# Hybrid decoder layer: dense units in another order, the convolution read from PSUM, and 21 slots for the expert stream instead of 19

## The chip, the cores and the metric

The kernel runs on one core of one Trainium2 chip. The metric is device time in microseconds (us) of one execution. TensorE (PE), VectorE (DVE), ScalarE (ACT) and GpSimd (POOL) compute; SyncE (SP) issues nearly all transfers from device memory. Each engine works through its own instructions in order and waits on semaphores.

## The reference, cut to what matters

One layer on 256 tokens of 1024 channels, float32 in and out:

```python
mod = silu(c) @ w_ada + b_ada                    # sh1, sc1, gt1, sh2, sc2, gt2
h = rmsnorm(x, norm1) * (1 + sc1) + sh1
q, k, v, ml_qk, ml_v, ml_o, ml_if, g_a, g_m = split(h @ w_in)
y_a = diff_attention(q, k, v)                    # 4 heads, softmax 0 minus lam * softmax 1, causal, ALiBi
qk = silu(sum(xp[:, j:j + S] * conv_w[j] for j in range(4)) + conv_b)   # causal, over time
h_t = mlstm(*split(qk), ml_v, gates)             # 4 heads
y_m = rmsnorm(sigmoid(ml_o) * h_t, mlstm_norm)
merged = sigmoid(g_a) * (y_a @ w_br_a) + sigmoid(g_m) * (y_m @ w_br_m)
x = x + gt1 * (merged @ w_out)
h2 = rmsnorm(x, norm2) * (1 + sc2) + sh2
# router: best of 4 groups, in it the best 2 of 8 experts; expert: w_e2 @ (silu(w_e1 h2) * (w_e3 h2))
x = x + gt2 * hier_moe(h2)
return rmsnorm(x, norm_f)
```

All weights are read once: the layer moves 164 MB, 100 MB of it for the 32 experts.

## The kernel before, in words

**Units.** All weights travel as units of 1 MB (128 partitions x 2048 float32), listed by `unit_list` (lines 55 to 69): 16 for the first phase (`mod` and `block`, 768 KB, in turn), then 40: `ada(i)` is a sixth of `w_ada` in four units, the rest are dense matrices. Each goes to a fixed slot of a ring of ten (`place`), and SP issues it once the last user of that slot is done (line 428). 96 expert units follow, eight quads of four experts, 12 units a quad: w1, w3, w2 of each. The first 19 go to slots freed by named jobs (`RELEASES`, lines 127 to 130), which include homes other than the ring (`late`, `qkT`, `gm`, `mqk`, `hT`, three spare tiles of `his`). Each later one waits until `used` counts one more consumed unit (line 440) and goes to the slot that comes next in the same cycle.

**Dense products** run in two rounded halves. For a dense unit d, ScalarE writes the high part (`split(d)`, line 502: 128 x 2048, one instruction), GpSimd subtracts it from the weight in four parts of 512 columns (line 478), and TensorE multiplies three times: high by high, low by high, high by low (`product`, line 1306: 48 products for a unit). `proj_T` and `proj` are its two layouts; `ml` is the mLSTM's q/k input (four units), `mv` its values, `mo` its output gate, `ga` and `gm` the branch gates. Three tiles hold high parts, so split(d) waits for unit d-3 to be consumed. `ada` (line 1259) is a float32 product of the conditioning vector in four column groups.

**Order by hand.** There is no planner: each engine's block lists its work. TensorE, from the end of the first phase: `if`, scores(0), ada(3), ifT, scores(1), ml0, scores(2), ml1, scores(3), ada(4), ml2, ml3, `cols` and `Mb` (the mLSTM's decay terms, which wait for `grows`), mv0, transposes of attention heads 0 and 1, mv1, `rb`, ada(2), times_v, mo0, mo1, ga0, ga1, gt1 spread, the mLSTM with ga2 and ga3, gm, branches, ada(5), `wo`, router. ScalarE's block has the splits between its own work: split(8), split(9) and split(10) around the copy of the four q/k banks (line 535); then for each head the exps, the copy of `ml` from its bank into `raw` and split(11 + h). VectorE's block: lam, scores and combine by head (lines 884 to 899), with conv(0) before combine(2) and conv(1) before combine(3), `cols`, conv(2), conv(3). A job in PSUM takes the next of eight banks in the order of `JOBS`, and its first product waits until the bank's last job is released.

**Convolution.** conv(i), lines 907 to 910: for each of two channels groups one TENSOR_SCALAR (last tap and bias), then three multiply-adds of `raw` shifted by one to three columns into `mqk`, each waiting for the one before.

**Experts.** quad(): up w1 (line 1644), gather half 0 of the next quad's tokens (line 1612), scatter the last quad's outputs into four accumulator banks (line 1601), gather half 1, up w3, transposes of the gate matrix and hidden values (lines 1619, 1622), down w2 (line 1656) into two banks. up runs four experts in turn on four column groups of the array; down runs two pairs of experts one after the other:

```python
for pair in ((0, 1), (2, 3)):
    wt = {e: arrived("w2", e, r, j) for e in pair}
    for c in range(2):
        for f in range(2):
            for e in pair:
```

The accumulators start as x (four products with the identity, line 1690), issued between the two gathers of the first quad.

## Time and profile before

| | us |
|---|---|
| median of 3 runs | 498.64 (496.84 to 499.54) |
| profiled execution | 499.77 |
| its span, first to last instruction | 497.9 |
| busy PE / DVE / ACT / POOL | 424.3 / 180.8 / 181.1 / 159.0 |
| mean granted clock of TensorE | 0.926 |
| DMA | 164.32 MB, mean 330 GB/s |

Busy times are unions of an engine's instructions, so a busy TensorE may still run at its lower clock: the granted clock is 1.00 at 2.4 GHz and 0.50 at 1.2 GHz. In rows of a timeline the columns are start, duration, engine, line, operation, output and inputs, count; brackets hold the idle time just before and what ended it.

### The profile page before, as it was taken

How to read it: one execution, taken by the hardware profiler on the slowest of the kernel's cores; microseconds unless marked ns; L12 is line 12 of the kernel's file. 1: busy time of each engine (PE TensorE's matmuls, PEld its weight loads, DVE VectorE, ACT ScalarE, POOL GpSimd, SP SyncE). 2: the span in 40 equal slices, each digit the busy share in tenths (PEclk: the TensorE clock that was granted, in tenths of full speed). 3: DMA queues.
4: the chain of work that ended last, by engine and by line, in shares of the span. 5: the costliest groups of instructions: out<-in, count | busy, mean ns of one | idle time of the engine just before them, and what ended most of it. 6: DMA issues, size and time to landing. Idle time of an engine off the chain costs nothing.

```text
span 497.9 us, 8612 instructions
## 1 busy us (share of the span) xinstructions
PE 424.3 (85%) x3612; PEld 317.9 (64%) x3612; DVE 180.8 (36%) x365; ACT 181.1 (36%) x332; POOL 159.0 (32%) x126
## 2 busy tenths in 40 slices
PE   6599459998599999999997989898989788584983
PEld 5599328898399999997996645363626254251531
DVE  0987027999661422357236011111111111102014
ACT  4676145654258357543343321212122112030122
POOL 0799074877335775997600000000000000000000
PEclk9799859999599999999996999898989889799799
DMA  8999988794096427477998299999999999999932
GB/s 296 424 419 421 422 352 355 280 378 168 9 406 223 151 105 254 170 274 318 424 420 339 74 387 423 421 421 420 421 420 421 421 423 420 421 423 419 419 157 86
DMA packets 23657, 164.32 MB, mean 330 GB/s; under 512 B 2624, under 2 KB 2752, under 8 KB 4928
## 3 DMA queue, kind: packets, MB, share of 16 engines
q1 hardware_dynamic: 23184, 162.15, 80.3%
q10 hardware_dynamic: 432, 1.57, 0.9%
q8 instruction: 31, 0.51, 0.4%
q14 instruction: 10, 0.08, 0.0%
HBM read 162.67 MB, written 1.05 MB: 329 GB/s over the span
## 4 chain that ended last, share of the span: by engine, by line
PE 59%; DMA 20%; DVE 14%; ACT 3%; issue 2%; SPq 1%; DVEq 0%; ACTq 0%
PE bank L1306 13%; PE cs_b L1644 10%; PE bank L1656 7%; PE cs_b L1306 7%; DMA ring<-in_rest 7%; PE bank L1612 6%; DMA hT<-in_e 6%; DMA his<-in_e 6%; PE bank L1601 4%; DVE mqk L910 3%; PE bank L1259 2%; PE bank L1349 2%; DMA ring<-in_mod 2%; DVE xn L897 1%; PE cs_b L1601 1%
## 5 line engine op out<-in xcount | busy, mean ns | idle before, releaser
L478 POOL TENSOR_TENSOR ring_r<-ring,his_r 128x512 fp32r<-128x512 f32 x120 | 158.6, 1357 | 74.7 <-ACT his_r L502 74.7
L715 ACT ACTIVATE raw<-bank,sm 128x128 f32<-128x128 f32 x72 | 27.1, 457 | 160.1 <-PE bank L1612 160.1
L502 ACT ACTIVATE his_r<-ring 128x2048 fp32r<-128x2048 f32 (+1 forms) x32 | 57.6, 1798 | 42.7 <-DMA ring<-in_rest 23.9
L1644 PE MATMUL cs_b<-ring,raw 128*32 128x256 f32 x544 | 58.5, 405 | 2.5 <-DMA ring<-in_e 2.5
L1185 DVE TENSOR_TENSOR tmp<-cs_b,tmp 128x256 f32<-128x256 f32 x8 | 3.4, 425 | 122.6 <-ACT tmp L723 122.6
L1612 PEld LDWEIGHTS bank<-const,xn 128*128 128x128 f32 x288 | 35.9, 199 | 9.0 <-issue 7.8
L1644 PE MATMUL cs_b<-his,raw 128*32 128x256 f32 x208 | 36.1, 420 | 5.5 <-DMA hT<-in_e 5.5
L1656 PE MATMUL bank<-ring,WT 128*32 128x512 f32 x128 | 39.2, 657 | 1.5 <-DVE WT L1190 1.5
L1644 PEld LDWEIGHTS cs_b<-ring,raw 128*32 128x32 f32 x544 | 29.4, 116 | 16.9 <-issue 6.3
L1612 PE MATMUL bank<-const,xn 128*128 128x128 f32 x288 | 37.7, 286 | 1.1 <-DVE const L1136 1.1
L1196 DVE TENSOR_TENSOR v<-bank,att 128x512 f32<-128x512 f32 x16 | 10.3, 687 | 48.1 <-PE bank L1656 48.1
L1306 PE MATMUL bank<-his_r 128*128 128x256 f32 x192 | 27.4, 286 | 0.0
L1601 PE MATMUL bank<-v,const 128*128 128x512 f32 x54 | 24.7, 594 | 1.7 <-DVE sm L1216 1.7
L1306 PEld LDWEIGHTS bank<-his_r 128*128 128x128 f32 x192 | 24.5, 190 | 1.1 <-issue 1.1
L1259 PE MATMUL bank<-ring,sm 128*32 128x256 f32 x256 | 18.7, 456 | 7.5 <-DVE sm L941 7.5
L1644 PEld LDWEIGHTS cs_b<-his,raw 128*32 128x32 f32 x208 | 16.8, 120 | 10.2 <-issue 8.6
L910 DVE SCALAR_TENSOR_TENSOR mqk<-raw,const,mqk 128x256 f32<-128x256 f32 x24 | 21.9, 913 | 0.9
L1656 PE MATMUL bank<-his,WT 128*32 128x512 f32 x56 | 19.7, 633 | 1.6 <-DVE WT L1190 1.6
L1259 PEld LDWEIGHTS bank<-ring,sm 128*32 128x32 f32 x256 | 9.1, 130 | 16.3 <-DVE sm L941 7.6
L1306 PE MATMUL cs_b<-his_r 128*128 128x256 f32 x128 | 18.4, 287 | 1.0 <-ACT his_r L662 1.0
L1656 PEld LDWEIGHTS bank<-ring,WT 128*32 128x32 f32 x128 | 9.4, 119 | 15.3 <-issue 13.0
L1644 PE MATMUL cs_b<-mqk,raw 128*32 128x256 f32 x48 | 13.0, 432 | 6.3 <-DMA his<-in_e 6.3
(385 smaller groups left out, 861.2 us busy)
## 6 DMA issues: line engine op xcount, KB each, us to landing
ring<-in_e SPq DMA_DIRECT2D x50, 1024.0 KB, 22.3
ring<-in_rest SPq DMA_DIRECT2D x40, 1024.0 KB, 7.0
his<-in_e SPq DMA_DIRECT2D x20, 1024.0 KB, 25.1
ring<-in_block SPq DMA_DIRECT2D x8, 768.0 KB, 21.3
late<-in_e SPq DMA_DIRECT2D x6, 1024.0 KB, 23.7
qkT<-in_e SPq DMA_DIRECT2D x5, 1024.0 KB, 18.7
mqk<-in_e SPq DMA_DIRECT2D x5, 1024.0 KB, 26.3
gm<-in_e SPq DMA_DIRECT2D x5, 1024.0 KB, 26.1
```

The lines of the kernel that those rows point to most:

```text
L478: pool.tensor_tensor(ring_r[:, slot_of(n), sl], ring[:, slot_of(n), sl], hi(d)[:, sl].bitcast(F32), ALU.subtract).then_inc(s["w_lo"], 1)
L502: act.activation(hi(d)[:, 0:WIDTH[d]], ring[:, slot_of(n), 0:WIDTH[d]], ACT.Copy).then_inc(s["w_hi"], 1)
L715: ins = act.activation(xg[:, b, k, :], token_bank[:, j * P:(j + 1) * P], ACT.Identity, bias=S("B2", KD)[:, k:k + 1], scale=S("A2", KD)[:, ...
L910: ins = dve.scalar_tensor_tensor(out=mqk[:, k, :], in0=raw[:, k, j:j + T], scalar=col("conv_w", 8 * j + k), in1=mqk[:, k, :], op0=ALU.mult ...
L1196: ins = dve.tensor_tensor(outs2[:, sl], out_banks[c][:], gt2b[:, sl], ALU.mult)
L1259: ins = pe.matmul(ps[32 * u:32 * u + 32, 0:256], S("cs", 8)[:, k:k + 1].to_broadcast([P, 32]), w[:, k - k0, 256 * u:256 * u + 256], start= ...
L1306: ins = pe.matmul(out, left(k), right(k), start=(i == 0 and k == 0), stop=(i == 2 and k == nk - 1))
L1349: ins = pe.matmul(pb(f"qk{i // 2}")[:, (i % 2) * T:(i % 2 + 1) * T], w[:, i * P:(i + 1) * P], h, start=start and i % 2 == 0, stop=stop, sk ...
L1601: ins = pe.matmul(y_banks[2 * tt + c][:], ptg[:, b, tt, :], outs2[:, 512 * c:512 * c + 512], start=False, stop=stop, skip_group_check=True)
L1612: ins = pe.matmul(token_bank[:, j * P:(j + 1) * P], xn[:, tt, k * P:(k + 1) * P], pone[:, tt].rearrange("p a n -> p (a n)"), start=(tt == ...
L1644: ins = pe.matmul(up_bank[e * CAP:(e + 1) * CAP, half], xg[:, b, k, e * CAP:(e + 1) * CAP], wt[e][:, k, :], start=(k == 0), stop=(k == KD ...
L1656: ins = pe.matmul(out_banks[c][e * CAP:(e + 1) * CAP, :], hidT[:, f, e * CAP:(e + 1) * CAP], wt[e][:, f, 512 * c:512 * c + 512], start=(f ...
```

## The change

- Units and TensorE's order: ml0 with scores(0) to ml3 with scores(3), ifT, mv0, mv1, ada(3), mo0, turn of ada(3), transposes of heads 0 and 1, `cols`, `Mb`, ada(4), mo1, times_v(0), (1), transposes of heads 2 and 3, ga0, times_v(2), (3), turn of ada(4), ada(2), ga1, `rb`; from the gt1 spread on as before. `JOBS` follows it.
- ScalarE and VectorE follow the new order (below). `scores` now has a buffer for each head (`sc` fills all of `att`), the mixes' factor on the second softmax goes to ScalarE (`scale`), and `wts` and `aT` move to `raw`, which is free.
- The convolution's last tap and bias are ScalarE's (`tap`, from the bank); its other three taps are VectorE's, with the bank as the first input. `raw` and its zero pad are no longer used for it.
- At the start normalize(0) goes ahead of modulation(0), and VectorE squares the last quarter of x.
- Two more slots for the expert stream: `OG` (the buffer of `o` with the gt1 spread next to it), freed when the squares of the new x are taken (`sq2`), and the home of x, freed when the normalized copy is made (`x2n`) and the accumulators hold x (`y_set`). The accumulators' four products go ahead of the gt2 spread.
- down() waits for all four w2 units and takes four experts in turn.

```diff
-    units = [u for k in range(KD) for u in (("mod", k), ("block", k))] + ada(3)
-    units += w_in(C_MQK, 2) + ada(4) + w_in(C_MQK + 512, 2)
-    units += w_in(C_MV, 2) + ada(2) + w_in(C_MO, 2) + w_in(C_GA, 4)
-    units += w_in(C_GM, 4)
+    units = [u for k in range(KD) for u in (("mod", k), ("block", k))]
+    units += w_in(C_MQK, 4) + w_in(C_MV, 2) + ada(3) + w_in(C_MO, 1) + ada(4) + w_in(C_MO + 256, 1)
...
+XSLOTS = SLOTS + 7
 YSLOTS = 16
...
-             (HT, "lg")]
+             (HT, "lg"), (OG, "sq2"), (X_HOME, "x2n")]
...
+        o_att = sb("o_att", [4096])
+        o, att = o_att[:, 0:1024].rearrange("p (t n) -> p t n", t=TT), o_att[:, 1024:4096]
         WT = sb("WT", [2, 384])
...
-        sc = att[:, 0:1536].rearrange("p (b c n) -> p b c n", b=2, c=2)
+        sc = att[:].rearrange("p (h c n) -> p h c n", h=HEADS, c=2)
...
                 return late[:, 0:UNIT]
+            if i == OG:
+                return o_att[:, 0:UNIT]
...
-                if n == NFIRST:
+                if n == NFIRST + 1:
...
-                elif job:
+                elif job == "sq2":
+                    sp.wait_ge(s["sq2"], 1)
+                elif job == "x2n":
+                    sp.wait_ge(s["x2n"], TT)
+                    sp.wait_ge(s["y_set"], 1)
+                else:
                     sp.wait_ge(*full(job))
                 load(slot_of(NPRE + m), m // QU, m % QU)
...
-                    act.wait_ge((xT0_in, xT1_in)[i // 2], 16)
+            for i in range(3):
+                act.wait_ge((xT0_in, xT1_in)[i // 2], 16)
...
-            split(9)
             for i in range(4):
                 act.wait_ge(*full(f"qk{i}"))
                 release(act.activation(qkT[:, 2 * i:2 * i + 2, :], pb(f"qk{i}")[:].rearrange("p (a n) -> p a n", a=2),
...
+            split(9)
+            act.wait_ge(s["lam_e"], 1)
+            act.activation(S("lexp", 2), S("ldot", 2), ACT.Exp).then_inc(s["lexp"], 1)
...
+                    act.activation(mqk[:, k, :], pb(f"ml{i}")[:, a * T:(a + 1) * T], ACT.Identity, bias=col("conv_b", k),
+                                   scale=col("conv_w", 24 + k)).then_inc(s["tap"], 1)
...
+                    act.activation(sc[:, h, 1, a:b], sc[:, h, 1, a:b], ACT.Identity, bias=0.0,
+                                   scale=S(f"rZl{h}", 2)[:, i:i + 1]).then_inc(s["sc1"], 1)
...
+            for h in range(HEADS):
+                tap(h)
+                split(10 + h)
+                exps(h)
+            split(14)
+            act.wait_ge(s["gates"], 2)
+            act.activation(grow[0:4, 2, :], grow[0:4, 2, :], ACT.Exp).then_inc(s["gexp"], 1)
+            act.wait_ge(s["gexp"], 1)
+            act.activation(grow[0:4, 2, :], grow[0:4, 2, :], ACT.Ln, bias=1.0).then_inc(s["gln"], 1)
+            scale(0)
+            scale(1)
+            values(0)
+            split(15)
+            scale(2)
+            values(1)
+            split(16)
+            scale(3)
+            output_gate(0)
+            split(17)
...
+            output_gate(1)
+            split(18)
             copy_a(2)
-            split(17)
             copy_a(3)
...
+            dve.wait_ge(xT1_in, 16)
+            dve.tensor_tensor(squares[:, 6:8, :], hT[:, 6:8, :], hT[:, 6:8, :], ALU.mult).then_inc(s["sq_d"], 1)
+            dve.wait_ge(*full("ss"))
+            release(dve.tensor_scalar(r1b, pb("ss")[:, 0:T], 1.0 / D, EPS, ALU.mult, ALU.add), "ss")
+            dve.wait_ge(s["std"], 1)
+            link(dve.reciprocal(r1b, r1b))
+            normalize(0)
...
             modulation(0, 0)
...
             modulation(0, 1)
...
+                    dve.wait_ge(s["sc1"], 2 * h + i + 1)
+                    dve.scalar_tensor_tensor(out=a_sb[:, h, a:b], in0=sc[:, h, 0, a:b], scalar=S(f"rZ{h}", 4)[:, i:i + 1],
+                                             in1=sc[:, h, 1, a:b], op0=ALU.mult, op1=ALU.add).then_inc(s["a_r"], 1)
...
+                dve.wait_ge(s["tap"], 2 * i + 2)
+                for a in range(2):
+                    k, seq = 2 * i + a, pb(job)[:, a * T:(a + 1) * T]
                     for j in range(3):
-                        ins = dve.scalar_tensor_tensor(out=mqk[:, k, :], in0=raw[:, k, j:j + T],
-                                                       scalar=col("conv_w", 8 * j + k), in1=mqk[:, k, :],
+                        back = 3 - j
+                        ins = dve.scalar_tensor_tensor(out=mqk[:, k, back:T], in0=seq[:, 0:T - back],
+                                                       scalar=col("conv_w", 8 * j + k), in1=mqk[:, k, back:T],
                                                        op0=ALU.mult, op1=ALU.add)
...
+                release(ins, job)
+
+            for h in range(HEADS):
+                conv(h)
+                scores(h)
+            gate_inputs()
+            dve.wait_ge(s["lexp"], 1)
+            link(dve.tensor_tensor(S("nlam", 1), S("lexp", 2)[:, 1:2], S("lexp", 2)[:, 0:1], ALU.subtract))
+            link(dve.tensor_scalar(S("nlam2", 1), S("nlam", 1), -LAMBDA_INIT, None, ALU.add))
+            sums(0)
+            sums(1)
+            mix(0)
+            sums(2)
+            mix(1)
             rows(3)
-            scores(0)
-            gate_inputs()
+            gate_sums()
+            sums(3)
+            mix(2)
+            mix(3)
...
-            scores(1)
-            combine(0)
-            scores(2)
-            gate_sums()
-            combine(1)
-            rows(4)
-            scores(3)
-            conv(0)
-            combine(2)
-
...
+            rows(4)
+            columns(A2, 4)
...
-            conv(2)
-            conv(3)
...
-            scores(0)
-            ada(3)
+            for h in range(HEADS):
+                proj_T(f"ml{h}", hsrc, next_dense(8))
+                if h == 0:
+                    for i in range(4):
+                        pe.wait_ge(*free(f"qk{i}"))
+                scores(h)
             ps = take("ifT")
             pe.wait_ge(*free("if"))
...
-            scores(1)
+            proj("mv0", hsrc, next_dense(8))
+            proj("mv1", hsrc, next_dense(8))
+            ada(3)
+            proj("mo0", hsrc, next_dense(8))
             ada_turn(3)
-            proj_T("ml0", hsrc, next_dense(8))
-            scores(2)
-            proj_T("ml1", hsrc, next_dense(8))
-            scores(3)
-            ada(4)
-            proj_T("ml2", hsrc, next_dense(8))
-            proj_T("ml3", hsrc, next_dense(8))
-            ada_turn(4)
...
+            transpose_a(0)
+            transpose_a(1)
...
-            proj("mv0", hsrc, next_dense(8))
-
+            ada(4)
+            proj("mo1", hsrc, next_dense(8))
...
-            transpose_a(0)
-            transpose_a(1)
-            proj("mv1", hsrc, next_dense(8))
...
+            po = [take("o0"), take("o1")]
+            times_v(0)
+            times_v(1)
+            transpose_a(2)
+            transpose_a(3)
+            gate_a(0)
+            times_v(2)
+            times_v(3)
+            ada_turn(4)
+            ada(2)
+            gate_a(1)
...
-            ada(2)
-            po = [take("o0"), take("o1")]
-            times_v(0)
-            times_v(1)
-            transpose_a(2)
-            proj("mo0", hsrc, next_dense(8))
-            transpose_a(3)
-            times_v(2)
-            proj("mo1", hsrc, next_dense(8))
-            times_v(3)
...
+            for job in ("x2T1", "wo3", "x2T2", "x2T3"):
+                pe.wait_ge(*free(job))
+            for tt in range(TT):
+                for c in range(2):
+                    ins = pe.matmul(y_banks[2 * tt + c][:], ident, x[:, tt, 512 * c:512 * c + 512], start=True, stop=False,
+                                    skip_group_check=True)
+            ins.then_inc(s["y_set"], 1)
             ada_spread(5, 2, 0)
             ada_spread(5, 2, 1)
...
-                for pair in ((0, 1), (2, 3)):
-                    wt = {e: arrived("w2", e, r, j) for e in pair}
-                    for c in range(2):
-                        for f in range(2):
-                            for e in pair:
-                                ins = pe.matmul(out_banks[c][e * CAP:(e + 1) * CAP, :], hidT[:, f, e * CAP:(e + 1) * CAP],
-                                                wt[e][:, f, 512 * c:512 * c + 512], start=(f == 0), stop=(f == 1),
-                                                tile_position=(0, e * CAP))
-                                if c == 1 and f == 1:
-                                    ins.then_inc(used, 1)
+                wt = [arrived("w2", e, r, j) for e in range(QUAD)]
+                for c in range(2):
+                    for f in range(2):
+                        for e in range(QUAD):
+                            ins = pe.matmul(out_banks[c][e * CAP:(e + 1) * CAP, :], hidT[:, f, e * CAP:(e + 1) * CAP],
+                                            wt[e][:, f, 512 * c:512 * c + 512], start=(f == 0), stop=(f == 1),
+                                            tile_position=(0, e * CAP))
+                            if c == 1 and f == 1:
+                                ins.then_inc(used, 1)
...
-            start_y(0)
             pe.wait_ge(s["g_evac"], 1)
             gather(1)
-            start_y(1)
```

## Rows read from the trace of the kernel before

**Rows 1.** The page, part 2: busy share of DMA in 40 slices of the span

```profile
DMA  8999988794096427477998299999999999999932
```

**Rows 2.** Windows: us, busy PE, PEld, DVE, ACT, POOL (count), clock, DMA share, GB/s

```profile
54.00:162.00 108.00, 88.16 (x792) 76.50 (x791) 67.15 (x123) 55.13 (x101) 59.01 (x46) 0.89 0.71 283
162.00:262.00 100.00, 98.34 (x850) 95.87 (x849) 37.79 (x67) 48.28 (x75) 67.14 (x51) 0.99 0.69 266
262.00:279.00 17.00, 14.41 (x64) 10.32 (x66) 8.21 (x45) 6.36 (x16) 0.00 (x0) 0.73 0.56 233
272.00:283.00 11.00, 11.00 (x96) 6.69 (x96) 1.61 (x6) 4.29 (x9) 0.00 (x0) 0.89 0.02 6
283.00:478.00 195.00, 165.71 (x1531) 88.82 (x1529) 25.58 (x56) 35.74 (x79) 0.00 (x0) 0.92 1.00 414
```

**Rows 3.** Timeline of TensorE

```profile
68.09 0.55 PE L1392 MATMUL cs_b<-qkT 64*128 64x128 f32 x1 [12.36 <-ACT qkT L535]
...
90.45 3.66 PE L1259 MATMUL bank<-ring,sm 128*32 128x256 f32 x64
...
129.60 5.62 PE L1259 MATMUL bank<-ring,sm 128*32 128x256 f32 x56 [7.48 <-DVE sm L941]
```

**Rows 4.** Chain of waits: start, duration, what

```profile
69.75 5.29 PE bank L1259 x64
75.05 4.92 DMA ring<-in_rest
...
129.60 6.05 PE bank L1259 x64
...
156.31 5.72 PE bank L1306 x48
...
278.97 3.65 PE cs_b L1644 x64
...
433.60 27.58 DMA his<-in_e
...
480.59 5.43 PE bank L1656 x32
```

**Rows 5.** Timeline of ScalarE

```profile
60.67 1.91 ACT L502 ACTIVATE his_r<-ring 128x2048 fp32r<-128x2048 f32 x1 [11.69 <-DMA ring<-in_rest]
```

**Rows 6.** Timeline of all engines at the start

```profile
14.54 1.75 DVE L827 RECIPROCAL tmp<-tmp 128x256 f32<-128x256 f32 x1
...
16.33 2.55 DVE L811 TENSOR_TENSOR hT<-hT,tmp 128x512 f32<-128x512 f32 x2
...
18.04 1.19 PE L1349 MATMUL bank<-his_r 128*128 128x256 f32 x4 [6.26 <-ACT his_r L520]
```

**Rows 7.** Windows, columns as in rows 2

```profile
79.70:82.10 2.40, 2.40 (x22) 2.40 (x21) 2.29 (x7) 2.10 (x2) 0.11 (x1) 1.00 1.02 430
...
129.50:133.10 3.60, 3.50 (x36) 1.66 (x40) 2.16 (x9) 3.09 (x9) 0.00 (x0) 0.50 0.00 0
```

**Rows 8.** Timeline of GpSimd

```profile
81.99 10.30 POOL L478 TENSOR_TENSOR ring_r<-ring,his_r 128x512 fp32r<-128x512 f32 x8 [9.50 <-ACT his_r L502]
...
102.60 5.43 POOL L478 TENSOR_TENSOR ring_r<-ring,his_r 128x512 fp32r<-128x512 f32 x4 [3.37 <-ACT his_r L502]
```

**Rows 9.** Timeline of VectorE

```profile
89.95 0.56 DVE L884 SCALAR_TENSOR_TENSOR att<-cs_b,const 128x384 f32<-128x384 f32 x1
...
104.08 4.23 DVE L910 SCALAR_TENSOR_TENSOR mqk<-raw,const,mqk 128x256 f32<-128x256 f32 x3
...
136.51 1.53 DVE L910 SCALAR_TENSOR_TENSOR mqk<-raw,const,mqk 128x256 f32<-128x256 f32 x3
```

**Rows 10.** Timeline of all engines before the first quad

```profile
268.52 3.78 PE L1612 MATMUL bank<-const,xn 128*128 128x128 f32 x16 [1.08 <-DVE const L1136]
...
272.09 3.06 PE L1690 MATMUL bank<-x,const 128*128 128x512 f32 x4
...
274.98 1.95 PE L1612 MATMUL bank<-const,xn 128*128 128x128 f32 x16
```

175 lines of the change are left out of this document (63 added, 112 removed).

## The prediction, made before the changed kernel ran

> **What bounds the kernel now.** I read the page first, then windows by stage, then the chain of waits, then the timelines of the places that the chain names. The DMA line of the page [rows 1] is to be read as three parts: full at the left, half empty in the middle, full from about 283 us on. The windows [rows 2] say what fills each part. From 54 to 162 us TensorE works 88.16 of 108 us at a granted clock of 0.89: time is lost here. From 162 to 262 us it works 98.34 of 100 us: nothing but less work would shorten this, and whatever is saved ahead of it is carried through. From 262 to 279 us the router leaves it gaps and a clock of 0.73. From 272 to 283 us DMA moves nothing (share 0.02), and from 283 to 478 us it is full (share 1.00, 414 GB/s) while TensorE is busy 165.71 of 195 us: the expert stream is bound by DMA. The chain agrees: its last DMA piece ends at 461.2 us, and behind it lie one quad's TensorE work and the final norm [rows 4]. So the end is: when the stream restarts, plus the units still to be moved, plus this tail.
>
> In the lossy stretch the timeline of TensorE shows two holes [rows 3]: 12.36 us before scores(0), released by ScalarE's copy of the q/k banks, and 7.48 us before ada(2), put down to the copy of `cols` on VectorE. ScalarE came late because its in-order queue stood 11.69 us at split(8) for the landing of ml0's weights [rows 5], which were fetched behind the four ada(3) units. VectorE came late because convolution and attention mixes lie ahead of `cols` in its order. After both holes the clock is at its lower level: ada(3) took 5.29 us and ada(2) 6.05 [rows 4], where ada(4), with no hole before it, took 3.66 [rows 3].
>
> **The change, part by part.**
>
> *Start.* normalize(0) goes ahead of modulation(0), which now waits behind sum, root and reciprocal. On VectorE: reciprocal from 12.7 instead of 14.54 us (1.75), one normalize (half of 2.55), then both modulations (2 x 1.2, by their spacing in time), and ScalarE's 1.1 us to the first hi tile: first product at 18.9 to 19.5 us, now 18.04 [rows 6]. The first six-bank pass is bound by TensorE from there on, so this is +1.0 us. Bounds: -0.5 (if the earlier square on VectorE and the shorter hole help) and +1.5.
>
> *Order of the dense units.* ml0 to ml3, mv0, mv1 come first, ada(3), ada(4), ada(2) later. ml0 now lands four units (10 us) earlier, before ScalarE asks for it at 50 us (it landed at 60.7 [rows 5]); the q/k copies stand ahead of split(9); TensorE goes from the `if` product straight to ml0, whose low part GpSimd has ready at 57 us. The hole of 12.4 goes and with it the cold clock behind it (1.7 on ada(3), 0.7 on scores(0)). In the ml part a head costs TensorE 5.72 [rows 4] + 0.9 = 6.6 us; VectorE six conv steps of 0.5 plus the scores' 2.3 [rows 7] = 5.3; ScalarE two taps, a split of 1.91 [rows 5] and four exps = 4.6; GpSimd 5.2 to 5.4 for a low part [rows 8]. All fit, GpSimd by half a microsecond. Attention then runs well ahead: I get `grows` on VectorE at about 104.4 us and `cols` on TensorE at 105.5, so the hole of 7.5 and its cold clock (2.4 on ada(2)) go too. Together -24.7 us.
>
> What is late next: split(17) (ga1) stands ahead of copy_a(0) on ScalarE. ga1's slot is freed by the end of ada(4), a landing in an idle queue takes 4.92 [rows 4], the split 1.91, the copy 0.5: 7.4 us, in which TensorE does mo1 (5.72). A hole of 1.7 us before times_v(0). Then copy_a(2) stands behind eight exps (ScalarE works 3.09 in the window 129.5 to 133.1 [rows 7]), two table loads and split(18): 9.0 us, against 7.8 of TensorE's work: a hole of 1.2. +2.9 us together (0 to 8: a wait behind the queue of each split). Behind these, o, rb and gt1 are ready about 1.4 us before TensorE wants them. VectorE now waits in columns(A2) for the turn of ada(4), 15 us earlier in its queue than the turn comes; behind it stand rows(2), o's scaling and rbias, none needed before ada(2) ends.
>
> *Convolution from PSUM.* ScalarE writes the last tap and bias, VectorE adds three taps read from the bank; the pad, the copy into `raw` and eight TENSOR_SCALARs go. Trace: three conv steps on `raw` in SBUF took 4.23 us (1.40 each) while GpSimd worked, 1.53 (0.51 each) when it no longer did; the 128x384 scores from PSUM took 0.56 at 89.95 us, beside a busy GpSimd [rows 8, 9]. I take 0.5 for a step, bounds 0.42 and 1.40 (a rival, below). The Trainium skill's page "VectorE: DVE Perf Modes", section "Rules for kernel authors", speaks against the edit: for elementwise work on a matmul's output accept the slow mode or, with many operations, copy to SBUF first; its table's fixed term for a PSUM source is 62 cycles above that for SBUF, by which I estimate 0.06 us x 24 = 1.6 us lost on VectorE. By it VectorE needs 5.7 of a head's 6.6 us, which leaves the sum and makes small waits likelier. The rows show the SBUF source dearer by 0.9 us a step as soon as GpSimd works; with 0.5 VectorE has 1.3 us to spare per head.
>
> *The accumulators' start.* The four x products (3.06 us for the first two, which the trace records as four, cold [rows 10]; 0.86 each warm) go from between the gathers to ahead of the gt2 spread, into time in which TensorE waits for the router; the rank product may come 0.3 to 0.5 us later for it. From 268.5 us there now follow gather(0) 3.78, x products, gather(1) 1.95, up at 278.97: 10.45 us [rows 10]. After: 0.3 + gather 1.8 + evacuation 1.5 + gather 1.8 + evacuation 1.5 + turn 0.45 + five hand-overs of 0.1 = 7.8 with a warm clock, 11.3 with both gathers cold. I take -2.2; bounds -2.7 and +1.
>
> *21 slots.* The stream restarts at the first `used`, close to 283 us, with 19 of 96 units loaded, and DMA stands still from 272 us [rows 2]. Two more units (OG freed by the last squares, x by x2n and the accumulators' start, both about 262 to 269 us) land in this hole: 5 us of work in 11. The stream after the restart has 75 units, not 77; a unit (1.05 MB) at 414 GB/s [rows 2] is 2.53 us: -5.1 us. Bounds -5.1 and 0 (if the end is not the stream's).
>
> *down() over four experts.* Its 32 products took 5.43 us in pairs [rows 4]. The same columns in groups of four, as up has them (64 x 256 columns in 3.65 us [rows 4]), give 3.7. Only the last quad's lies behind the stream: -1.7. In exchange it waits for all four w2; DMA still trickles at 479 to 480 us and down starts at 480.59, so I allow +0.3 (bounds -1.7 and +1.0). In the other quads the stream hides it.
>
> **Sum.** +1.0 - 24.7 + 2.9 - 2.2 - 5.1 - 1.7 + 0.3 = -29.5 us. The profiled execution took 499.77 us (span 497.9), 1.1 above the median of 498.64; against its own time that gives 470.3. I say 470.
>
> **Rivals.**
> *Small waits in the dense stretch.* The ten units now run with 0.5 to 1 us between what GpSimd, ScalarE and TensorE need. If each is late by a microsecond the stretch gives back 10 us: 480. For: GpSimd took 1.36 a part beside a busy VectorE [rows 8], and its work follows ScalarE's split, which follows the tap. Against: the dense units after 162 us ran with TensorE busy 98.34 of 100 us [rows 2].
> *The extra slots bring nothing:* the transfer was hidden anyway, or the first quads' TensorE work paces the restart. 475. Against: DMA is full from 283 to 478 us without a gap.
> *Conv from PSUM is held up like conv from SBUF.* 24 x 1.40 = 33.6 us on VectorE instead of 12; `grows` then comes at about 125 us, TensorE waits 20 us at `cols` and runs cold for 2.4: 492. For: one input and the output are still in SBUF. Against: the scores' row at 89.95 [rows 9]. The Trainium skill's page "SBUF — State Buffer", section "Who interferes with whom", has it that a VectorE instruction with at most one SBUF input, outside the two-port modes, does not contend with GpSimd; that row agrees (0.56 us), and by the page alone I would give this rival half of the chance below.
> *Slower: ScalarE's queue waits for landings.* split(15) and split(17) now stand ahead of the copies that TensorE needs, each for weights whose slot was freed only a moment before. With a landing of L us the first costs L - 10 beyond what is hidden, the second L - 3. At 4.92 this is the 1.7 above. In a full queue landings take 22 to 28 us (his<-in_e 27.58 [rows 4]); from L = 22 on the two cost 31 us and the whole gain is gone; at 28 it is 43, so 511. Against: between 110 and 140 us DMA is a third busy. It decides at L = 22.
>
> **How the numbers follow.** Forecast 0.62, small waits 0.15, slots without effect 0.10, conv held up 0.09, slower 0.04. The forecast's own range, with the bounds of start, holes and router, is 465 to 476. The time should lie in 464 to 482, which leaves out conv held up, the slow case and the worst of the small waits. A measurement of this kernel tells about 0.5% (2.5 us) from no change; faster by more than that 0.94, within it 0.02, slower 0.04.
>
> **What would show it.** First product near 19 us; no TensorE hole above 3 us from 20 to 140 us and a clock of 1.00 there; conv steps near 0.5 us with GpSimd busy; short holes before times_v(0) and times_v(2), each released by ScalarE; ga1's product ending near 139 us, up of the first quad at 256 to 258; the two extra loads landed before DMA restarts at about 260; last w1 wait ending near 433 to 435; down in 3.7 us. The prediction is wrong if a hole of over 5 us stands anywhere before 140 us, if conv steps take over 1 us, or if the stream's restart is not followed by 186 to 190 us of full DMA.

## The result, and the profile after

The changed kernel took 475.78 us (473.49 to 477.03, four runs), the kernel before beside it 499.09: a ratio of 0.953, 95% interval 0.947 to 0.959. Six further runs of the same kernel beside 11 of the one before gave 0.951 (0.949 to 0.954). The forecast was 470 with a range of 464 to 482. The profiled execution was the slowest of the four, 477.03 us (span 475.2); a second profile, from the further runs, took 473.88 (span 472.0). Both are used below, since they differ in one place and that place matters.

The page of the changed kernel: the header, and the busy share of DMA in 40 slices (to be held against [rows 1]).

```profile
PE 404.6 (85%) x3612; PEld 310.7 (65%) x3612; DVE 168.3 (35%) x350; ACT 187.6 (39%) x344; POOL 157.2 (33%) x125
...
DMA  8999998579887455479998899999999999999912
```

The gap before the full part at the right has closed: no slice under 8 is left behind the middle, where before there was a 2. The windows by stage say the same (columns as in [rows 2]):

```profile
54.00:143.00 89.00, 86.99 (x800) 76.42 (x799) 48.40 (x102) 60.88 (x115) 52.93 (x43) 0.98 0.82 323
143.00:244.00 101.00, 98.10 (x851) 95.46 (x850) 45.64 (x75) 46.12 (x73) 66.93 (x51) 1.00 0.71 277
244.00:259.00 15.00, 10.72 (x63) 7.99 (x62) 8.21 (x45) 7.06 (x17) 0.00 (x0) 1.00 1.01 421
259.00:263.00 4.00, 4.00 (x68) 2.61 (x67) 1.27 (x3) 1.00 (x1) 0.00 (x0) 1.00 0.13 47
263.00:460.00 197.00, 157.26 (x1568) 87.34 (x1567) 27.14 (x60) 37.68 (x81) 0.00 (x0) 0.93 0.97 400
```

The lossy stretch of [rows 2] (108 us with 88.16 us of TensorE's work, clock 0.89) is now 89 us with 86.99 of work at 0.98. The router's stretch is at full clock, 0.73 before. DMA all but stands still for 4 us (share 0.13), not for 11. From DMA's restart to the end of the last down it is 197 us; before it was 203, from 283 [rows 2] to 486.0 [rows 4].

The timeline of TensorE, at the places of [rows 3], and the two holes that were forecast in their place:

```profile
96.66 3.66 PE L1280 MATMUL cs_b<-ring,sm 128*32 128x256 f32 x64
...
109.20 5.30 PE L1280 MATMUL cs_b<-ring,sm 128*32 128x256 f32 x64
...
121.81 0.46 PE L1464 MATMUL bank<-v,raw 128*128 128x128 f32 x2 [1.40 <-ACT raw L603]
...
130.37 0.49 PE L1464 MATMUL bank<-v,raw 128*128 128x128 f32 x2 [0.61 <-ACT raw L603]
...
132.12 3.66 PE L1280 MATMUL cs_b<-ring,sm 128*32 128x256 f32 x64
...
153.46 0.46 PE L1510 MATMUL cs_b<-late,WT 128*128 128x129 f32 x2 [1.24 <-issue]
```

Here 64 products of `ada` (L1280) stand in the first, second and fifth row, 2 products of attention with v (L1464) in the third and fourth. The holes of 12.36 and 7.48 us are gone. Two small ones before the products with v came as foreseen. Two things did not: ada(4), the second row, ran at the lower clock (5.30) with no hole ahead of it, and there is a hole of 1.24 us ahead of the first numerator.

Timelines of VectorE and GpSimd. The first two rows are six steps of the convolution each, 0.51 us a step, for the first and the second head; the third is GpSimd's row of subtractions, which starts at 65.81 us and so stands beside the last two of the first six steps only. The fourth row is eight small scalings of the router's weights, 1.0 us each on the mean (six of them took 1.3 us, beside a busy GpSimd); in the kernel before, the fifth row, the same eight took 1.28 us together, because GpSimd was idle just then.

```profile
63.96 3.07 DVE L933 SCALAR_TENSOR_TENSOR mqk<-cs_b,const,mqk 128x253 f32<-128x253 f32 x6 [3.24 <-ACT mqk L545]
...
71.21 3.06 DVE L933 SCALAR_TENSOR_TENSOR mqk<-bank,const,mqk 128x253 f32<-128x253 f32 x6 [1.96 <-ACT mqk L545]
...
65.81 5.03 POOL L483 TENSOR_TENSOR ring_r<-ring,his_r 128x512 fp32r<-128x512 f32 x4 [2.67 <-ACT his_r L507]
...
143.66 8.04 DVE L996 TENSOR_SCALAR const<-const,sm 128x36 f32<-128x36 f32 x8
```

```profile
144.09 1.28 DVE L965 TENSOR_SCALAR const<-const,sm 128x36 f32<-128x36 f32 x8
```

These eight now stand in front of gate 1's spread and of the decay that the numerator reads: that is the new wait.

The two rows of convolution start 7.25 us apart, and so do the next two, while a head takes TensorE 6.78 us. ScalarE's tap of the next head stands behind the exps of this one, the exps wait for VectorE's scores, the scores stand behind the convolution, and the convolution waits for the tap. So ScalarE and VectorE form a round of 7.25 us, though VectorE is busy for only 5.0 us of it and ScalarE for 4.7, and TensorE's distance from them shrinks by half a microsecond a head.

Ahead of the first quad, in place of [rows 10] (timeline of TensorE): the x products first, then two gathers with nothing between them but their evacuations, all at the upper clock. The first `up` starts at 259.19 us, 278.97 before.

```profile
244.16 2.82 PE L1603 MATMUL bank<-x,const 128*128 128x512 f32 x6
...
251.44 2.05 PE L1635 MATMUL bank<-const,xn 128*128 128x128 f32 x16 [1.08 <-DVE const L1157]
...
255.10 2.05 PE L1635 MATMUL bank<-const,xn 128*128 128x128 f32 x16 [1.60 <-ACT raw L741]
```

The end, as the chain of waits shows it (start, duration, what). Down of the last quad now waits for a landing, and takes 3.74 us:

```profile
429.59 26.62 DMA his<-in_e
...
456.35 3.74 PE bank L1678 x32
...
461.42 0.17 DVE sm L1237
461.59 1.76 issue
463.35 4.51 PE bank L1624 x6
467.85 0.87 PE cs_b L1624 x2
```

Down ends 26 us earlier than before, and the span is only 22.7 us shorter. Behind VectorE's last instruction stand 1.76 us in which TensorE waits for nothing that the profile shows, and six of the last scatter's products then take 4.51 us, most of them at the lower clock. The second profile of the same kernel has at this place:

```profile
461.10 0.17 DVE sm L1237
461.26 0.14 issue
461.40 1.97 PE bank L1624 x4
```

0.14 us and the upper clock (2.81 us for the six). So these 3 us belong to one execution and not to the change: in the 13 other profiles of this document this place has 0.15 to 0.82 us and 2.81. Why TensorE stood still in this one isn't shown; that its instructions came late is a guess.

### The profile page after: what moved, and what is told of

It reads as the page before. It is cut to its first block, busy times and chain, and to the rows that moved or that the text cites. A ratio compares the mean times of both kernels' runs of the same rounds, so it can differ in the third digit from the quotient of the medians.

```text
span 475.2 us, 8601 instructions
## 1 busy us (share of the span) xinstructions
PE 404.6 (85%) x3612; PEld 310.7 (65%) x3612; DVE 168.3 (35%) x350; ACT 187.6 (39%) x344; POOL 157.2 (33%) x125
## 4 chain that ended last, share of the span: by engine, by line
PE 66%; DMA 20%; ACT 4%; DVE 4%; SPq 3%; issue 2%; DVEq 0%; ACTq 0%
PE bank L1327 17%; PE cs_b L1327 9%; PE cs_b L1667 8%; DMA gm<-in_e 6%; DMA ring<-in_e 6%; DMA his<-in_e 6%; PE bank L1370 5%; PE bank L1635 5%; PE bank L1678 5%; PE bank L1624 4%; SPq L441 3%; PE cs_b L1280 3%; PE bank L1375 2%; DMA hT<-in_xT 2%; PE cs_b L1624 1%
## 5 line engine op out<-in xcount | busy, mean ns | idle before, releaser
L1667 PE MATMUL cs_b<-ring,raw 128*32 128x256 f32 x544 | 51.2, 401 | 6.7 <-DMA ring<-in_e 6.7
L1678 PE MATMUL bank<-ring,WT 128*32 128x512 f32 x112 | 30.3, 693 | 4.8 <-DMA gm<-in_e 3.2
L1327 PE MATMUL bank<-his_r 128*128 128x256 f32 x208 | 29.8, 286 | 0.0
L1217 DVE TENSOR_TENSOR v<-bank,o_att 128x512 f32<-128x512 f32 x16 | 10.3, 686 | 41.3 <-PE bank L1678 41.3
L1667 PE MATMUL cs_b<-his,raw 128*32 128x256 f32 x176 | 23.9, 394 | 0.0
L1667 PE MATMUL cs_b<-late,raw 128*32 128x256 f32 x64 | 17.8, 442 | 4.6 <-DMA ring<-in_e 4.6
L1327 PE MATMUL bank<-his_r,ring_r 128*128 128x256 f32 x144 | 20.2, 283 | 0.0
L1327 PE MATMUL bank<-hT_r,his_r 128*128 128x256 f32 x144 | 19.9, 280 | 0.0
L1624 PEld LDWEIGHTS bank<-v,const 128*128 128x128 f32 x54 | 10.0, 198 | 13.5 <-issue 13.5
L1327 PEld LDWEIGHTS bank<-his_r,ring_r 128*128 128x128 f32 x144 | 18.6, 192 | 0.0
L1327 PEld LDWEIGHTS bank<-hT_r,his_r 128*128 128x128 f32 x144 | 18.3, 189 | 0.0
## 6 DMA issues: line engine op xcount, KB each, us to landing
ring<-in_block SPq DMA_DIRECT2D x8, 768.0 KB, 21.5
```

What stands on the lines that cost most here:

```text
L1217: ins = dve.tensor_tensor(outs2[:, sl], out_banks[c][:], gt2b[:, sl], ALU.mult)
L1327: ins = pe.matmul(out, left(k), right(k), start=(i == 0 and k == 0), stop=(i == 2 and k == nk - 1))
L1624: ins = pe.matmul(y_banks[2 * tt + c][:], ptg[:, b, tt, :], outs2[:, 512 * c:512 * c + 512], start=False, stop=stop, skip_group_check=True)
L1667: ins = pe.matmul(up_bank[e * CAP:(e + 1) * CAP, half], xg[:, b, k, e * CAP:(e + 1) * CAP], wt[e][:, k, :], start=(k == 0), stop=(k == KD ...
L1678: ins = pe.matmul(out_banks[c][e * CAP:(e + 1) * CAP, :], hidT[:, f, e * CAP:(e + 1) * CAP], wt[e][:, f, 512 * c:512 * c + 512], start=(f ...
```

## The experiments

Twelve runs; a median is over all executions of a kernel; a difference "against the changed kernel" is that of the two ratios to the kernel before, times 498.3 us, and is good to about 1.5 us. In each run one execution was profiled, and it need not be a typical one.

**The changed kernel once more.**

> The changed kernel itself, again, to stand beside the others on one chip. Its four times so far were 473.5, 474.6, 477.0 and 477.0 us, its profiled execution 477.0. Expected: a median of 474 to 477. Theory A (the last scatter sometimes runs at the lower clock): the times fall into two groups about 2 to 3 us apart, and a profile of the faster group has the last scatter's six products at about 2.8 us instead of 4.5. Rival B: one group, and the spread is noise of the transfers.

Measured: 474.2 us; five of six between 472.7 and 476.2, one of 480.3. The profile has the last scatter at the upper clock, as theory A has it for a fast execution, but the times don't fall into two clean groups, and no other profile has the late scatter: it is a rare source of the spread, beside others.

**Down in pairs again.**

```
-                wt = [arrived("w2", e, r, j) for e in range(QUAD)]
+                for pair in ((0, 1), (2, 3)):
+                    wt = {e: arrived("w2", e, r, j) for e in pair}
```

> The changed kernel with only down() back in pairs of experts, 32 products where two at a time run beside each other instead of 16 steps of four. Theory A (the forecast's term, -1.7 us, was given back in the tail): down takes 5.3 to 5.4 us in each quad again, the last quad's end comes 1.7 us later, but the gap between the end of VectorE's last work and the final scatter shrinks from 1.8 us to about 0.3 and the scatter runs at the upper clock, so the time is the same within 1 us or up to 1.6 us less. Rival B (the tail's gap has nothing to do with down): the gap of 1.8 us and the scatter of 4.5 us stay and the time rises by 1.7 us.

Measured: 475.6 us, ratio 0.954 (0.952 to 0.956): 1.5 us more, which is just the size that these comparisons resolve. The last down took 5.38 us and TensorE no longer waited for a landing in front of it. That fits rival B's number, though not its mechanism: there was no gap that down could have hidden. The surer evidence is the rows themselves, 5.38 against 3.74 us behind the stream. The last scatter stood right behind VectorE's last instruction and ran at the upper clock, as in the changed kernel's second profile.

```profile
467.06 2.81 PE L1624 MATMUL bank<-v,const 128*128 128x512 f32 x6 [1.69 <-DVE sm L1237]
```

In the middle quads pairs took 7.05 us and a quad 24.0, groups of four 3.64 and 20.6. Of these 3.4 us only half are the pairs': the 7.05 us have a granted clock of 0.76, where the last quad's 5.38 and the 3.64 have 1.00. All of it was hidden, as forecast: the stream needs 29.8 us for a quad, and the groups of four simply wait longer.

**19 slots.**

```
-XSLOTS = SLOTS + 7
+XSLOTS = SLOTS + 5
-             (HT, "lg"), (OG, "sq2"), (X_HOME, "x2n")]
+             (HT, "lg")]
```

> The changed kernel with 19 expert slots: the two last ones (the attention output's buffer with the spread gate, and x) are left out. Theory A (the stream of expert weights sets the end, and 8 transfers or so were missing between the last early one and the first freed slot): the DMA engines idle again from about 255 to 263 us, the last transfer ends 4.3 to 5.1 us later and the time rises by as much. Rival B (slots bring nothing, the order of the dense units did it all): the time is the same within 0.5 us.

Measured: 480.1 us, ratio 0.963 (0.961 to 0.965): 5.9 us more. The windows from 244 to 272 us show where: first the changed kernel (its second profile), then the one with 19 slots. The last two columns are DMA share and GB/s; everything ahead of this window is equal to 0.6 us.

```profile
244.00:272.00 28.00, 23.70 (x200) 17.02 (x203) 9.61 (x50) 11.37 (x25) 0.00 (x0) 1.00 0.84 346
```

```profile
244.00:272.00 28.00, 23.70 (x176) 16.33 (x178) 9.49 (x48) 9.76 (x22) 0.00 (x0) 0.94 0.61 245
```

101 GB/s less over 28 us is 2.8 MB, the two units (2.1) and the later restart. Theory A holds; the rival of slots without effect is out. The clock of 0.94 is another matter: in this profile the x products ran at the lower clock and the first `up` came 1.1 us later for it (see the start undone, below), so part of the profile's difference isn't the slots'.

**The convolution's input in SBUF.**

```
-                    k, seq = 2 * i + a, pb(job)[:, a * T:(a + 1) * T]
+                    k, seq = 2 * i + a, const[:, CONSTS["ident"][0]:CONSTS["ident"][0] + T]
```

> The changed kernel, its convolution's 24 steps on VectorE reading 256 columns of the constants in SBUF (identity and ones) instead of the product in PSUM; so the convolution is not computed, and everything else is. Theory A (a step whose input lies in PSUM isn't held up by GpSimd's subtractions, one with all its operands in SBUF is): the steps go from 0.51 us to 1.0 to 1.4 us each, 24 of them cost 12 to 21 us more on VectorE between 63 and 92 us, the products of the attention scores wait for their banks, TensorE gets holes of 5 us and more before the gates' columns, and the time rises by 8 to 18 us. Rival B (the source doesn't matter, the steps were slow before because they ran at another moment): 0.5 us each and the same time.

Measured: 481.8 us, ratio 0.967 (0.965 to 0.970): 7.9 us more. The steps by their source line, shortest, median and longest in ns, first with PSUM (18 of the 24 steps), then with SBUF (all 24); below them the group with SBUF with its mean, and GpSimd's row beside the first head:

```profile
L933 DVE SCALAR_TENSOR_TENSOR mqk<-bank,const,mqk x18: 479/481/484, 71.2 to 88.3; 128x253 f32<-128x253 f32 x6, 128x254 f32<-128x254 f32 x6, 128x255 f32<-128x255 f32 x6
```

```profile
L933 DVE SCALAR_TENSOR_TENSOR mqk<-const,mqk x24: 481/484/1400, 62.5 to 93.3; 128x253 f32<-128x253 f32 x8, 128x254 f32<-128x254 f32 x8, 128x255 f32<-128x255 f32 x8
L933 DVE SCALAR_TENSOR_TENSOR mqk<-const,mqk 128x253 f32<-128x253 f32 (+2 forms) x24 | 18.9, 786 | 9.8 <-ACT mqk L545 9.1
64.38 5.44 POOL L483 TENSOR_TENSOR ring_r<-ring,his_r 128x512 fp32r<-128x512 f32 x4 [2.68 <-ACT his_r L507]
```

The mean of 786 ns is no size of a step. Of each head's six steps the first four end before or just as GpSimd starts and take 0.48 us, with either source; the last two stand wholly beside it and take 1.37 to 1.40 us from SBUF and 0.48 from PSUM. At the same place in the same kernel the source is the cause. Theory A's mechanism and its size for a held-up step (1.0 to 1.4) hold; what it had wrong is the number of such steps, 8 and not 24. The way to TensorE was another one too. The round of ScalarE and VectorE grows by 1.8 us, from 7.25 to 9.1 (the convolutions start at 62.54, 71.64, 80.71 and 89.79 us), ScalarE's split comes late with it, and TensorE then waits for GpSimd's low part:

```profile
78.93 1.58 PE L1327 MATMUL bank<-his_r,ring_r 128*128 128x256 f32 x8 [1.92 <-POOL ring_r L483]
97.11 1.21 PE L1327 MATMUL bank<-ring_r,his_r 128*128 128x256 f32 x8 [2.04 <-POOL ring_r L483]
```

From the first product to the attention output's transposes this profile is 4.7 us longer than the changed kernel's second one, and its time, 478.7 us, is 4.8 longer; it was the fastest of its four executions. What made the others 480.7 to 483.1 isn't shown.

**The router's scalings later.**

```
-            for k in range(KD):
-                dve.tensor_scalar(w_r[:, k, :], w_r[:, k, :], A2[:, k:k + 1], None, ALU.mult).then_inc(s["wr_r"], 1)
...
             hidden(3)
+            for k in range(KD):
+                dve.tensor_scalar(w_r[:, k, :], w_r[:, k, :], A2[:, k:k + 1], None, ALU.mult).then_inc(s["wr_r"], 1)
```

> The changed kernel with VectorE's eight scalings of the router's weights moved from before the spread of gate 1 to behind the last hidden(), where the next consumer on TensorE is 25 us away. Theory A (the eight, 1.0 us each beside GpSimd's subtractions, make the first numerator late): the hole of 1.24 us ahead of the first numerator goes, the transposes of the attention output start at 162.0 instead of 163.2 to 163.8, and the time falls by 1.2 to 1.5 us, 0.3 per cent, which a median of five rounds may just tell. Rival B (the numerator waits for something else, such as the exponentials of the decay on ScalarE): the hole stays. If the scalings in their new place hold up the normalization of the hidden state, a hole appears ahead of its transposes at about 190 us.

> The kernel with the late scalings alone once more: its profiled execution was the fastest seen (472.3 us), and its others lay between 476 and 491. Theory A (a disturbance while it ran): now 471 to 475 in all. Rival B (the edit opens a second, slower course of the execution, such as a landing just missed): again some executions above 480 us.

Measured: the hole ahead of the numerator went. It starts at 151.62 us in a profile whose first product is at 18.59; in the changed kernel's second profile these are 154.01 and 18.96, so the gain is 2.0 us there, and the transposes of the attention output come 2.1 us earlier. Part of this is the clock of ada(4), which was quick here: against the three profiles with the scalings at their old place and a quick ada(4) (19 slots, start undone, accumulators between the gathers) the gain is 0.9 to 1.9 us at the two places. Yet the two series gave medians of 481.1 and 481.7 us. Three of the 12 executions took 471.7, 472.3 and 476.4 us, the other nine 478 to 491. Rival B of the second expectation is right in that a second, slower course exists, though it is not a landing. The mean granted clocks of the two profiled executions are 0.955 and 0.950, so the clock isn't it. The two profiles, one of a short and one of a long execution, show the same two instructions of VectorE, the low parts of the hidden state for the output projection:

```profile
188.84 3.22 DVE L1048 TENSOR_TENSOR qkT_r<-qkT,raw_r 128x512 fp32r<-128x512 f32 x2 [17.16 <-ACT raw_r L680]
```

```profile
189.90 16.40 DVE L1048 TENSOR_TENSOR qkT_r<-qkT,raw_r 128x512 fp32r<-128x512 f32 x1 [17.15 <-ACT raw_r L680]
```

One instruction of 0.7 us took 16.40 us. In the long execution's windows VectorE has its two instructions and nothing else for 16.3 us, GpSimd is busy 15.25 of them, and TensorE is idle for half:

```profile
190.50:206.80 16.30, 7.87 (x68) 7.67 (x66) 16.30 (x2) 4.36 (x3) 15.25 (x13) 0.90 0.50 194
```

```profile
206.96 1.22 PE L1327 MATMUL bank<-raw_r,his_r 128*128 128x256 f32 x4 [8.59 <-DVE qkT_r L1048]
```

VectorE's instruction ended only when GpSimd had run out of work. GpSimd's subtractions took 1.24 us each in that run (18 in 22.38 us), 1.38 in the changed kernel (21 in 29.07 us): there the two engines took turns. Over all fourteen profiles the pair took 3.2 us in seven, 7.0 in four, 17.0 in three. Only the 17.0 reach TensorE: from the attention output's transposes to the turn of the new x it takes 69.1 us with a pair of 3.2 or 7.0 (69.7 in the short profile here) and 79.1 to 79.2 with one of 17.0.

The move of the scalings changed where in GpSimd's row the pair is issued: 14.1 us behind its start instead of 15.3. At 15.3 the pair took 3.2 or 7.0 (ten profiles), at 14.1 it took 3.2 once and 17.0 three times. So the place fits the longer median. But it doesn't decide alone: the short and the long profile above are of one program, with the pair at the same place. Nor does the distance from the start of GpSimd's current subtraction, 0.29 to 0.30 us in the seven long cases and 0.27 to 0.34 in the seven short ones, one of them at 0.29. What decides stays open; no run varied the moment alone, and a version that reads these inputs from PSUM, which the convolution's steps suggest, was not tried.

**The copies ahead of the splits.**

```
             output_gate(0)
-            split(17)
...
             copy_a(0)
             copy_a(1)
+            split(17)
...
-            split(18)
             copy_a(2)
             copy_a(3)
+            split(18)
```

> The changed kernel with ScalarE's copies of the turned attention weights (two and two) ahead of the splits that stood before them, whose weights land late (101 and 119 us). Theory A (ScalarE's queue waits for landings in front of the copies that the products with v need): the holes of 1.4 to 1.5 and 0.6 us ahead of the first and third product with v go, both, and what follows comes 2.0 us earlier: the time falls by 2 us. If ada(4) now ran at the upper clock too, 1.6 us more would be gained, since it is no longer hidden by the landing. Rival B (TensorE only meets its next wait: GpSimd's low parts of the next unit are late by as much, since the split waited for the same landing): the holes move to the products of the gate, and the time stays.

Measured: 475.7 us, ratio 0.955 (0.952 to 0.959): no gain, if anything 2 us more (1.1 us of it in this profile, from x products at the lower clock before the first `up`). The hole before the first product with v went (117.78 us instead of 121.8), the one before the third stayed at 1.25, and all of it came back where the previous experiment would look for it:

```profile
140.20 9.70 DVE L996 TENSOR_SCALAR const<-const,sm 128x36 f32<-128x36 f32 x8
```

```profile
151.66 0.46 PE L1510 MATMUL cs_b<-late,WT 128*128 128x129 f32 x2 [2.91 <-issue]
```

The eight scalings started 3.5 us earlier and took 9.7 us beside eight subtractions of GpSimd. Neither theory as written: the next wait was not a landing but the contended VectorE. This run also answers for the clock: ada(4) took 3.66 us here and in seven other profiles, 5.30 to 5.35 in four. Where it was short the hole behind it was longer (2.8 to 3.8 us instead of 1.4 to 1.5, this run's own order aside): the landing that the copies wait for did not come earlier. From the first product of the blocks to the first product with v it is 102.8 to 103.5 us with the slow ada(4) (the convolution from SBUF left aside) and 102.0 to 103.0 with the quick one and the old order of the copies, so its lower clock cost at most one microsecond.

**Both, and with the old start.**

> The changed kernel with both: the scalings of the router's weights behind the last hidden(), and the copies of the turned attention weights ahead of the splits. Alone, the copies removed the holes before the products with v but the time came back ahead of the first numerator, where the hole grew from 1.25 to 2.91 us. Theory A (there VectorE's contended scalings were the next wait): with both edits no hole over 1 us is left between 57 and 165 us, the transposes of the attention output start 4 to 5 us earlier than in the changed kernel (at 159 instead of 163.8), and the time falls by 3.5 to 5 us against it. Rival B (a landing is next: the stream of dense weights at full rate bounds this stretch): the hole appears at another product, released by GpSimd or ScalarE behind a DMA, and the gain stays under 2.5 us.

> The same two edits and the start as before the change. If the three add up: the start's 1 us more, the transposes of the attention output at 158, the time 5 to 6 us under the changed kernel's, 468 to 469 us. If landings bound the dense stretch, the start's 1 us is lost there and this equals the kernel with the two edits.

Measured: fastest executions 469.7 and 469.1 us, medians 479.6 and 477.8, five of six each time above 477. Up to 165 us theory A is right in its direction, and the gain is above its range: the transposes of the attention output at 157.74 and 157.52 us, 5.5 to 6.3 us earlier than in the changed kernel where it had 4 to 5, with one hole of 1.24 left where it had none over 1. Of the old start's 1 us only 0.2 are seen here. Then the same pair of VectorE instructions takes 17.0 us in both profiles. The fastest execution of the version with all three edits is 3.6 us below the changed kernel's fastest (472.7), and its median is about 3 us above; it does not beat the changed kernel.

**The start undone.**

```
-            dve.wait_ge(xT1_in, 16)
-            dve.tensor_tensor(squares[:, 6:8, :], hT[:, 6:8, :], hT[:, 6:8, :], ALU.mult).then_inc(s["sq_d"], 1)
-            normalize(0)
             dve.wait_ge(*full("cs0"))
             dve.wait_ge(*full("cs1"))
             modulation(0, 0)
+            dve.wait_ge(*full("ss"))
+            release(dve.tensor_scalar(r1b, pb("ss")[:, 0:T], 1.0 / D, EPS, ALU.mult, ALU.add), "ss")
             modulation(0, 1)
...
+            normalize(0)
```

> The changed kernel with the start as before: all four squares on ScalarE and the first modulation on VectorE ahead of the sum of squares' scaling. Theory A (the start costs 1.0 us in the changed kernel): the first product of the blocks starts at about 18.0 instead of 19.0 us, the product of the input gates ends 1.0 to 1.3 us earlier, and the time falls by 1.0 to 1.3 us. Rival B (the later start is paid back inside the eight blocks, where the modulations and landings set the pace): the end of the blocks and the time stay.

Measured: 473.3 us (472.0 to 475.2), ratio 0.950 (0.947 to 0.952): 0.8 us less, the fastest median of all, though within the measurement of the changed kernel. The first product starts at 17.34 us and not at 18.96, the transposes of the attention output at 161.94 and not at 163.79. VectorE's pair took 7.0 us instead of 3.2, which cost nothing: at the router's first product the lead is still 1.8 us (238.07 against 239.89). At the router's first gather (251.87 against 252.01) it was gone, because the x products took longer, here and in the changed kernel's second profile:

```profile
243.13 4.28 PE L1601 MATMUL bank<-x,const 128*128 128x512 f32 x6
```

```profile
244.73 2.82 PE L1603 MATMUL bank<-x,const 128*128 128x512 f32 x6
```

They ran at the lower clock, and the gt2 spread and the rank product stand behind them in TensorE's order. Four of the eleven profiles with the x products at this place have them so, the others not. From the router's first product to the first `up` it is 19.8 to 19.9 us in the seven others, 21.5 to 21.6 in three and 23.0 in the fourth. What brings the lower clock isn't shown.

The first product itself is no fixed landmark: it starts at 17.3 to 18.1 us in the four profiles with the old start and at 18.2 to 19.8 in the ten with the new one, the means 1.0 us apart.

**The accumulators' start between the gathers.**

> The changed kernel with the eight products that start the accumulators back between the two gathers, as before, the 21 slots kept (the load into x then waits for the second half of them). Theory A (ahead of the router's rank they cost nothing, between the gathers they stand on the path to the first quad): the first down starts 2.2 to 2.7 us later, the extra slot in x is released about 12 us later but still before the first weights are spent, and the time rises by about 2 us. Rival B (between router and stream there is slack, since the stream of the weights sets the end and its first freed slot comes from w1's products): the time rises by less than 1 us.

Measured: 474.8 us, ratio 0.954 (0.951 to 0.956): 1.3 us more. The timeline of TensorE shows a second reason beside the products' own time:

```profile
249.68 3.53 PE L1628 MATMUL bank<-const,xn 128*128 128x128 f32 x16 [1.08 <-DVE const L1157]
```

The first gather takes 3.53 us, at the lower clock, as it did in the kernel before (3.78 [rows 10]); in every profile with the products ahead of the router's rank it took 2.05. They fill time in which TensorE waited, though not without cost: in this run the rank product starts at 247.57 us, when VectorE releases it, and in the changed kernel it starts 0.7 us behind that moment. From the router's first product to the first `up` it is 20.85 us here, 1.0 more than with the x products ahead and at the upper clock, but 0.7 less than with them ahead and at the lower one. The gain was about half of the term.

**The kernel before with one edit.** ScalarE's four copies of q and k stand ahead of split(8) instead of behind split(9):

```
-                split(k + 1)
+                if k < KD - 1:
+                    split(k + 1)
+            for i in range(4):
+                act.wait_ge(*full(f"qk{i}"))
...
+            split(8)
             act.wait_ge(const2_in, 16)
             act.wait_ge(s["lam_e"], 1)
```

> The kernel before with one edit: ScalarE copies q and k out of PSUM ahead of the split that waits for the first dense unit's landing (60.7 us). The dense units' order and all else stay. Theory A (the hole of 12.4 us needed only this, but the rest of the stretch is paced by landings and by VectorE's convolution, so the order and the convolution have to change too): the attention scores start at about 57 instead of 68 us and the hole shrinks to 2 to 3 us, but the hole of 7.5 us ahead of ada(2), which waits for VectorE, grows by most of that, and the time falls by 0 to 5 us. Rival B (the order of queues was all there was to it): the whole 9 to 10 us stay gained, and the time is 488 to 489 us.

Measured: 492.0 us, ratio 0.988 (0.984 to 0.992), profiled execution 490.8. Timeline of TensorE:

```profile
65.97 1.86 PE L1404 MATMUL bank<-o,const 16*4 16x256 f32 x4 [5.17 <-DVE o L853]
...
101.81 0.66 PE L1272 MATMUL cs_b<-const,arow 128*128 128x128 f32 x2 [2.73 <-DVE arow L774]
```

The time lies between the two theories. The hole of 12.36 went, new ones of 5.17 and 2.73 us opened, the hole of 7.48 shrank to 0.46, and 8.6 us of lead over the kernel before are kept at the transposes of the attention output (171.75 against 180.31). Theory A was wrong in that the second hole grows: it shrank, because VectorE's attention work started earlier as well (its first scores at 67.28 us). One moved copy brings 9 us in the profile and 6 to 7 over all executions; the rest of the change, which no run takes apart here, brings the other 8.5 of the 17.1 us at this point.

## Why the prediction was right, point by point

*What bounds it.* Right. The 100 us of dense TensorE work carried the lead of 17.1 us from the attention output's transposes to the router's first gather without loss, the router's stretch added 2.7, and DMA was full from there on.

*Start, +1.0.* Measured 0.98 at the first product, 1.0 in the mean of all profiles, and 1.4 at the input gates' product; undoing it gave 0.8.

*Order, -24.7, and new holes, +2.9.* With the start these made -20.8 at gate 1's spread; measured -18.65 (143.22 against 161.87 us). The holes were forecast as 1.7 and 1.2; they are 1.40 behind an ada(4) that took 1.65 more, and 0.61. A head took 6.8 us and not 6.6, 0.7 over the four. With the start's 0.4 that places 1.8 of the 2.2 us; 0.3 I can't place. That the holes' removal needed the whole reorder was my silent assumption: half of the gain came with the one moved copy.

*The step that was wrong* stands under the same heading: "Behind it stand rows(2), o's scaling and rbias, none needed before ada(2) ends." rbias brought eight scalings with it that were not priced at all. Moved from beside an idle GpSimd to beside a busy one they went from 1.28 to 8.04 us together and stood ahead of gate 1's spread and the decay. Between gate 1's spread and the next landmark the lead fell from 18.65 to 17.1; the run without them there gained 2.0, or 0.9 to 1.9 against profiles with the same clock at ada(4).

*Convolution at 0.5 a step.* Measured 0.48, 0.51 from start to start. The rival's mechanism is real, and so is its 1.40 for a held-up step; but in the new order GpSimd works beside only 8 of the 24 steps, so it would have cost 8 us in all and not 22. What the Trainium skill's page "SBUF — State Buffer", section "Who interferes with whom", states, that a VectorE instruction with at most one SBUF input, outside the two-port modes, does not contend with GpSimd and one with two does, agrees with the two runs' rows, 0.48 against 1.40 us beside GpSimd. The cost that I estimated from the cycle table of the Trainium skill's page "VectorE: DVE Perf Modes" isn't seen: a step from PSUM took what one from SBUF took beside an idle GpSimd, 0.48 us in both runs.

*Small waits.* None on TensorE in the ml stretch, but not for the reason given. The prediction compared each engine's own work with TensorE's 6.6 us and had GpSimd as the tightest. GpSimd stood idle 2.2 us in each head; the tightest was the round of ScalarE and VectorE, 7.25 us, longer than TensorE's 6.78. Four heads are too few for the half microsecond that it loses on each to reach TensorE: here the forecast was lucky. With the held-up steps the round was 9.1 us, and it did.

*Router, -2.2.* -2.7 in the profile (278.97 to 259.19, less the 17.1); 1.3 of it by the experiment is the products' place, and all of that hangs on their running at the upper clock, which four of eleven profiles don't show.

*Slots, -5.1, down, -1.7 + 0.3.* Together -6.5; from DMA's restart to down's end it is 6 us less. By experiment 5.9 and 1.5, somewhat more than their places in the sum, each within its error. Down waits for its last weights as foreseen, 1.45 and 0.79 us in the two profiles.

*Together.* Against 470.3 the second profile's 473.9 leaves 3.6 us: 2.7 up to gate 1's spread (its lead there is 18.1 and not 18.65), 1.6 for the scalings, -0.5 for the router, -0.2 behind the first `up`. The first profile's 477.0 has 3.1 more, the standstill and the cold scatter at the end, which are the bad luck of an execution. The later landmarks came late by the same amounts: the first `up` at 259.2 us (256 to 258 forecast), the last wait for w1 ending at 436.5 (433 to 435). The slower rival decides at a landing of 22 us; the one in question took 4.67.

## What to carry to other kernels

When a block of work is moved, list every instruction that moves with it, and ask of each which other engine was idle at its old place and is busy at its new one: eight instructions of 1.28 us together became 8.04 us and stood in front of the next release. When engines hand work to each other in a ring, add up the ring and not each engine's share: engines that each fitted into 6.6 us made a round of 7.25. Where GpSimd streams subtractions over SBUF, a PSUM input kept VectorE's steps at 0.48 us instead of 1.40. When a mean stands between two known sizes, look at the single instructions. And before believing an edit by its profile, look at the spread of its executions: an edit that wins up to 2 us in the trace can move an instruction into a place where it starves, and lose 7 in the median.

## What the runs showed of the hardware

- A VectorE instruction with both inputs in SBUF (128x512, float32 to the rounded format) can wait for the whole of GpSimd's unbroken row of work: 0.68 us alone, 1.5 to 1.8, 5.33 or 16.40 beside it, in steps and not in between, and 1.5 as well as 16.40 in two executions of one program. The Trainium skill's page "SBUF — State Buffer", section "Who interferes with whom", has a VectorE instruction with two SBUF inputs contend with a GpSimd instruction that reads SBUF, over a shared pair of ports with an exclusive lock. These rows go further: the block lasted over 13 GpSimd instructions in a row, so nothing made them take turns.
- A VectorE instruction held up beside GpSimd's subtractions took about as long as one of these, whatever its own size: the 128x36 scaling 1.3 us instead of 0.23, the 128x253 step with two SBUF inputs 1.40 instead of 0.48. The same step with a PSUM input stayed at 0.48.
- TensorE's granted clock fell to its lower level (1.2 GHz) with no hole ahead in some profiles: 0.58 and 0.50 in the slices around 109 to 112 us, behind 3 us of transposes and products of four rows, while eight of the twelve profiles with these instructions kept 2.4 GHz there.
- The same 32 products of down took 5.38 us in pairs of two tiles and 3.64 in groups of four at the upper clock; in pairs with a granted clock of 0.76 they took 7.05.
